# Joining the routing programs and the expert programs of a decoder layer into one block

## The reference, cut to what matters

```
grp_p, grp_idx = lax.top_k(softmax(xt @ w_router_group + b), 1)      # one of 8 groups
top_p, top_local = lax.top_k(softmax(logits of that group), 2)       # two of its 8 experts
order = argsort(expert_id)                                           # rows of one expert together
...
hid = silu(xb @ w_gate[e]) * (xb @ w_up[e]);  y = hid @ w_down[e]    # 3 matrices of 2 MB each
out = x + gate2 * rms_norm(sum of the two weighted rows of y)
```

## Time and profile before

| | us |
|---|---|
| median of 3 runs | 2518.11 |
| lowest, highest | 2517.96, 2519.18 |
| the profiled execution | 2512.39 |
| its span, first to last instruction | 2510.4 |

### The profile page before, as it was taken

How to read it: one execution, slowest core, us unless ns; L and a number is a source line. 1 busy time by engine, 2 the same in 40 slices (tenths; PEclk the granted TensorE clock), 3 DMA queues, 4 the chain that set the end, 5 groups by cost and what they waited for, 6 DMA issues and landing times. The chain is left out here.

```text
span 2510.4 us, 49117 instructions
## 1 busy us (share of the span) xinstructions
PE 2390.8 (95%) x17719; PEld 1715.9 (68%) x17721; DVE 1290.2 (51%) x3699; ACT 759.4 (30%) x1739; POOL 438.5 (17%) x722
## 2 busy tenths in 40 slices
PE   6999999999999999999997799999999999899997
PEld 5778888988889888898875465565555455555453
DVE  1878898888988889888896300000000000000016
ACT  1324444344443444343433212212212111112124
POOL 0112221222212221122212301001001010001013
PEclk8999999999999999999999899999999999999999
DMA  9630000000000000000003999999999999999989
GB/s 365 252 118 36 17 34 17 34 32 19 26 26 34 17 34 20 31 34 17 34 19 117 391 415 417 428 427 428 424 417 428 413 420 420 401 427 405 407 362 401
DMA packets 81052, 550.03 MB, mean 219 GB/s; under 512 B 14157, under 2 KB 14557, under 8 KB 54122
## 3 DMA queue, kind: packets, MB, share of 16 engines
q1 hardware_dynamic: 58914, 389.00, 38.2%
q10 hardware_dynamic: 9704, 126.80, 11.9%
q0 software_dynamic: 12384, 33.57, 3.4%
HBM read 513.16 MB, written 47.71 MB: 223 GB/s over the span
## 5 line engine op out<-in xcount | busy, mean ns | idle before, releaser
L428 PE MATMUL pj_ps<-scratch,home 128*128 128x128 f32 x5120 | 611.9, 278 | 2.0 <-issue 2.0
L2238 PE MATMUL gate_up_ps<-home,scratch 128*64 (+1 forms) x1344 | 594.8, 600 | 0.0
L428 PEld LDWEIGHTS pj_ps<-scratch,home 128*128 128x128 f32 x5120 | 586.8, 192 | 11.4 <-issue 5.4
L1358 DVE SCALAR_TENSOR_TENSOR cvf<-cfpre,chp,cvf 128x128 f32<-128x128 f32 x1920 | 587.8, 368 | 12.4
L2236 PE MATMUL gate_up_ps<-longgu,scratch 128*64 128x512 f32 x992 | 439.6, 601 | 20.5 <-issue 12.9
L2380 DVE TENSOR_TENSOR scratch<-scratch,gate_up_ps 128x512 f32<-128x512 f32 x42 | 28.9, 687 | 597.7 <-PE gate_up_ps L2238 597.7
L2258 PE MATMUL y_ps<-home,scratch 128*64 (+1 forms) x672 | 296.9, 595 | 0.0
L2236 PEld LDWEIGHTS gate_up_ps<-longgu,scratch 128*64 128x64 f32 x992 | 136.0, 139 | 152.6 <-issue 47.4
L2384 DVE COPY scratch<-y_ps 128x512 f32<-128x512 f32 x84 | 58.1, 692 | 345.8 <-PE y_ps L2258 295.4
L2256 PE MATMUL y_ps<-longdn,scratch 128*64 128x512 f32 x496 | 218.6, 593 | 13.7 <-ACT scratch L2318 12.3
L652 PE MATMUL wide_ps<-home 128*128 128x512 f32 x496 | 219.5, 595 | 0.8 <-ACT home L982 0.8
(11 more groups left out here) (458 smaller groups left out, 2953.4 us busy)
## 6 DMA issues: line engine op xcount, KB each, us to landing
home<-in_w_gate_dram SPq DMA_DIRECT2D x43, 2048.0 KB
home<-in_w_up_dram SPq DMA_DIRECT2D x43, 2048.0 KB, 16.8
home<-in_w_down_dram SPq DMA_DIRECT2D x43, 2048.0 KB, 25.6
home<-in_w_ada_dram SPq DMA_DIRECT2D x12, 2048.0 KB, 11.6
home<-in_w_gate_dram ACTq DMA_DIRECT2D x10, 2048.0 KB
home<-in_w_up_dram ACTq DMA_DIRECT2D x10, 2048.0 KB, 34.5
home<-in_w_down_dram ACTq DMA_DIRECT2D x10, 2048.0 KB, 39.8
longgu<-in_w_gate_dram ACTq DMA_DIRECT2D x10, 2048.0 KB, 15.2
```

What stands on the lines that cost most here:

```text
L428: mm = pe.matmul(pj[bank][:, g % 4, :], t.win[:, k, col + (g % 4) * P:col + (g % 4 + 1) * P], hT[:, k, :], start=(k == 0), stop=(k == KD - 1))
L1358: ins = dve.scalar_tensor_tensor(cvf[:, g, :], src, w, cvf[:, g, :], ALU.mult, ALU.add)
L2238: mm = pe.matmul(out[short_side, :], xT[:, k, short_side], w, start=(k == 0), stop=(k == KD - 1))
```

## The change

`build_routing` becomes `routing_programs`, which builds no block. It returns one function for each engine, and `build_experts_and_combine` calls them at the head of its own engine programs. The bodies of the five functions are those of before, instruction for instruction and with the same waits between engines, with one addition for SyncE. The meeting at the end of routing is gone. In its place each engine that reads `info` waits for its last part (`info_known`), and SyncE waits for `table_ps` and `info_ready`, because the tiles of routing now lie in the second long slot (`slot1`) and in `G2`. The PSUM tiles of routing become views of `gate_up_ps`, `xT_ps` and `y_ps`.

```
-def build_routing(nc, r, t, dram):
+def routing_programs(r, t, dram):
...
+    def in_slot(*shape, dt=F32):
+        return view(r.slot1, big, shape, dt)
+    def in_row(*shape, dt=F32):
+        return view(r.G2, small, shape, dt)
...
-        V = sb("V", [P, NCH, NG, EPG])
-        MM, CC = (sb(n, [P, NCH, NG, EPG], BF16) for n in ("MM", "CC"))
+    V = in_slot(NCH, NG, EPG)
+    MM, CC = (in_slot(NCH, NG, EPG, dt=BF16) for _ in range(2))
+    rowoh, stepoh = in_slot(2 * NCH, P), in_slot(2 * NCH, STEPS + 2)
...
+    rk = r.gu_ps[:].rearrange("p a b -> p (a b)")
+    ip, cb = (r.x_ps[:, n, :] for n in range(2))
+    tb, busy = (r.y_ps[:, n, :] for n in range(2))
...
-        block = own.enter_context(nc.Block())
-        @block.sync
-        def _(sp):
+    def route_sync(sp):
         sp.wait_ge(info_ready, 1)
         short = short_expert(sp, r, 1)
         for m in range(3):
             sp.wait_ge(r.short_in[m], 16)
             load_short(sp, r, dram, m, short, 1)
+        sp.wait_ge(table_ps, 1)
+        sp.wait_ge(info_ready, 4)
...
+    def info_known(eng):
+        eng.wait_ge(info_ready, 4)
+    return route_sync, route_gpsimd, route_scalar, route_tensor, route_vector, info_known
```

In `build_experts_and_combine` (the loads behind `route_sync(sp)` are those that were there, `load_long` of the second long slot first):

```
+        r.gu_ps, r.x_ps, r.y_ps = gu_ps, x_ps, y_ps
-        G2, hp2 = sb("G2", [P, D]), sb("half_pow2", [P, 2])
+        G2, hp2 = r.G2, sb("half_pow2", [P, 2])
+        route_sync, route_gpsimd, route_scalar, route_tensor, route_vector, info_known = routing_programs(r, t, dram)
         block = own.enter_context(nc.Block())
         @block.sync
         def _(sp):
+            route_sync(sp)
...
             long = long_expert(sp, r, 1)
             for m in range(3):
                 load_long(sp, r, dram, m, long, 1)
...
+            route_gpsimd(pool)
+            info_known(pool)
...
+            route_tensor(pe)
+            info_known(pe)
             x_transposes(0, 0)
...
+            route_scalar(act)
+            info_known(act)
             x_evac(0)
...
+            route_vector(dve)
```

And in `build`:

```
-            build_routing(nc, r, t, dram)
-            r.longgu.append(sb(wts, "longgu1", [P, 2 * KD, DE]))
-            r.longdn.append(sb(wts, "longdn1", [P, KE, D]))
+            r.slot1, r.G2 = sb(wts, "long1", [P, SLOT]), sb(wts, "G2", [P, D])
+            r.longgu.append(r.slot1[:, 0:2 * KD * DE].rearrange("p (k f) -> p k f", f=DE))
+            r.longdn.append(r.slot1[:, 2 * KD * DE:SLOT].rearrange("p (k f) -> p k f", f=D))
             build_experts_and_combine(nc, r, t, dram)
```

More of the change, by code:

```diff
@@ L2496, in build @@
         t, r = Tiles(), Tiles()
-        t.ctx = ctx
+        t.ctx, t.nc = ctx, nc
         t.cst = sb(ctx, "cst", [P, C_MATS, P])
```

531 lines of the change are left out of this document (264 added, 267 removed).

## The result

Median of six runs each: 2525.12 us after (2521.44 to 2528.25), 2516.26 us before (2510.42 to 2519.18); the ratio is 1.0033, 95% interval 1.002 to 1.0046. The difference of the medians is 8.9 us, forecast was 7.4. The profiled execution took 2524.59 us, its span is 2522.7 us.

The account below looks back on a forecast made before the run. Bound by TensorE's and the loads' lines, almost equally fast. Meeting -0.1, gather +6.1, transposes +1.1, gate +0.3, rest 0 make 7.4 us, so 2518.11 becomes 2525.5 us; 8 times in 10 from 2519 to 2530.

Parts of the forecast that it names:

- The meeting itself: End of routing: GpSimd's DRAIN lasts as long as its gather, so removing the meeting gives 0.1 us, 0.4 at most.
- The gather behind the loads: First gather, behind three early loads: 10.8 us from issue to last packet against 4.75 alone, +6.1 us.
- Rival (c): First gather takes turns with the loads from its first packet: shift 3.5 us, 2521.6 us; chance 0.12.
- The clock: TensorE after the longer wait: transposes at half speed +1.1 us, first gate matmuls +0.3 us.
- The views and the waits: Routing tiles as views and the info_known waits: cost 0, from -0.1 to +0.3 us.
- The loads' lead: Loads issued earlier fill idle DMA time, but the lead is lost by 1510 us: return 0, at most 4.5 us.
- (a): At the meeting: pure cost, gather undisturbed; -0.4 us on TensorE, 2517.7 us if the lead is lost; chance 0.09.
- (b): Stretch 1713 to 2342 us: the loads' lead lives on, 4.9 to 6.7 us sooner, 2511.4 us; chance 0.06.
- (d): First gather waits as with two queues of loads beside it: 6 us more, 2531.5 us; chance 0.06.
- The sum: Whole kernel: all terms together 7.4 us slower, 2518.11 to 2525.5 us, 0.29%.
- the forecast's own range: Whole kernel: 2523.3 us (gather 2 us quicker) to 2529 us (1.7 us of clock and 1.8 us of gather on top).
- The sign of being wrong: Trace after: forecast wrong if transposes begin before 1420 us or the shift at 1513 us differs from the end's.

Follow-up runs that it names:

- e3: Against the kernel before: meeting and late loads kept, only the tiles as views as in the changed kernel; 2517.44 us, ratio 1.0005.
- e1: Changed kernel, but SyncE loads the second long slot only when the first gather has landed; 2515.74 us, ratio 0.9995 to the kernel before.
- e2: Kernel before with tiles as views, meeting kept, second long slot's three loads moved ahead of the meeting; 2525.41 us, ratio 1.0027.
- e4: Changed kernel with one of the three loads ahead of the gather and two behind its landing; 2521.48 us, ratio 1.0016 to the kernel before.
- e6: Changed kernel with 14 instead of 5 idle matmuls behind the table and 3 behind the first transposes; 2523.09 us, ratio 1.0023.
- e8: e7 with 10 instead of 8 idle matmuls ahead of the table and four short ones in the table's pauses; 2513.16 us, ratio 0.9981.
- e5: Changed kernel, but the second long slot's three loads wait for the first evacuation of the transposes (xT_ready); 2517.35 us, ratio 1.0002.
- e7: e1 with 7 instead of 5 idle matmuls behind the table and 3 behind the first transposes; 2516.21 us, ratio 0.9992.

## Why the prediction was right, by its own steps

- **The meeting itself: -0.1 us forecast, -0.4 measured** (from last packet to transposes, e3 against e1), the upper bound that the prediction gave. It took the end of the DRAIN, 1418.0, for the end of the gather; the last packet was there at 1417.6. That the meeting wasn't the late one is shown by e2.
- **The gather behind the loads: +6.1 forecast; 6.3 measured, issue to last packet 10.6 us against 4.3.** From issue to transposes it is 11.14 us, against 5.16 before and 4.58 in e1. The row taken for it, the second gather of the kernel before, gave 10.8 us for issue to last packet and was the right one. The late start and then the turns came as in the earlier trace rows. Rival (c), turns from the first packet on, falls, but it was priced wrongly: it took away the whole 3.9 us without a packet, of which 1.9 are there for a gather alone, too. Priced rightly it would have given some 5 us of shift and not 3.5, at the border of what the forecast calls slower. (The prediction once calls it the second rival; it is the third.) e1, e2 and e4 are the proof that it is the loads: taken away, put into the kernel with a meeting, and cut to a third.
- **The clock: +1.1 for the transposes and +0.3 for gate.** The transposes cost 0.8 us more (1.95 against 1.12). The gate stretch at half speed was no longer than before (3.4 us against 3.6), so this term was nothing, or 0.2 us the other way: from the first transpose to the product of step 0 the two together cost 0.6 us against 1.4 forecast. The traces of e6 to e8, at full clock there, put the whole matter at 2.3 us in the kernel after, of which 1.7 were already in the kernel before.
- **The views and the waits: 0.** e3 agrees within its interval, and e5's routing stage is as long as that before.
- **The loads' lead: 0.** It was lost before step 0 was over: the DMA engines stood still from 1434 to 1440 us. The forecast said 1431 to 1437, and everything lies 2.4 us later in this execution. Rivals (a), (b) and (d) fall with the 11.1 us of the trace after.
- **The sum: 7.4 us forecast.** In the pair of traces the steps of the prediction come to 6.0 + 0.6 = 6.6 us, at step 0 and still at step 17; the medians are 8.9 us apart. That the median forecast, 2525.5 us, lies 0.4 us from the measured 2525.12 is luck: the shift was forecast 1.5 us too small, and the median of three runs that it was added to lies 1.9 us above that of the six. (The lower end of the forecast's own range, 2 us below 2525.5, is 2523.5 and not 2523.3; nothing hangs on it.)
- **The sign of being wrong:** the shift at 1513 us was to be that of the end. In this pair it is not, 9.0 us at step 17 and 12.3 at the end. By the ten traces above the stretch behind step 17 varies by 5 us with or without early loads, so one pair can't test the sign; the step from TensorE's start to step 17 holds in all of them, the rest of the way is borne out by the medians alone.
- **Not foreseen:** in this pair of executions the table ends 2.4 us later (1413.42 against 1411.06 us), before the loads can act: 0.8 us from the end of the mixer, where the four records of L755 took 3.34 us instead of 1.88 (mean granted clock from 1360 to 1370 us 0.84 instead of 1.00), and 1.5 from the last 38 records of the table, 6.09 against 4.55 us (0.72 instead of 1.00). Both are the clock. It is not a cost of joining: e5, also joined, has 4.55 us, and e3, with the meeting, has 7.41 us for 48 records, more than full speed would need (48 x 0.12 = 5.8). Whether the tiles as views make it likelier is open: of the eight traces with views and the rests of the table unfilled, seven show the fall and e5 doesn't; of the kernel before there is one trace, and it doesn't either. By the time of e3 the views, with all that they bring, are worth 3.8 us at most. This may be why the medians differ by 1.5 us more than forecast, or chance may; the interval of the ratio, 1.002 to 1.0046, is 5 to 12 us and holds both figures.
- **Wrong in a detail:** the trace puts TensorE's wait down to "issue", not to the gather's DMA; what ended the wait has to be read from the queues.

## What to carry to other kernels

A meeting of the engines can be a guard that nobody wrote down: look at which DRAIN ends last and at what starts behind the meeting, for it will start earlier. Transfers that nobody needs yet should be issued behind the one that TensorE waits for, by a wait on its landing. And where a saving makes a queue start sooner, find the next place at which that queue runs dry; here a lead was worth nothing beyond it (1434 to 1440 us in the kernel after).

## What the runs showed of the hardware that I had not expected

GpSimd's DRAIN lasts until its own gather has landed: 4.97 us with the gather alone, 11.98 us behind 6 MB of loads (e2). A gather issued by GpSimd while loads run has no packet for 4.1 to 4.5 us, whether 2 MB or 6 MB are ahead of it (the second gather of the kernel before; the kernel after, e2, e4, e6); alone its first packet is there after 1.9 us. What makes the 2.2 to 2.6 us in between is open: no run here varies anything but the amount of the loads, and that made no difference. After that the packets alternate as by the turns between queues of the Trainium skill (DMA: Bandwidth & Descriptors, Queues, rings and completion order): 144 of the gather beside 156 of the loads in the kernel after. A packet is here what the profile counts as one, up to 4 KB of the gather and 16 KB of the loads, so the gather gets 0.41 of 2.67 MB in that stretch, about a sixth.

TensorE's granted clock fell to 1.2 GHz within the table in seven of the nine traces in which TensorE rests between its pieces, for 0.3 to 1.0 us, and ahead of the first. In the kernel before and e5, with the same rests between pieces, it stayed at 2.4 GHz. The rest ahead of the first piece was 0.95 and 0.87 us there, 1.2 us in e3 and 2.1 to 2.5 in the others; that it makes the difference is not shown. In e8, with the rests filled, the last piece ran at full speed; one trace doesn't show that the filling did it. Its 0.9981 against e7's 0.9992 is not resolved by itself, its gain over the kernel before is.
